# Expert layers in steps of four 32-row tiles instead of two 64-row tiles

## What is computed

```python
def hierarchical_moe(h, rg_w, rg_b, re_w, re_b, w_gate, w_up, w_down):
    x = h.reshape(-1, d)
    ...   # top-1 of 4 groups, then top-2 of 8 experts in it: two experts of 32 per token
    hid = silu(einsum("nd,edf->nef", x, w_gate)) * einsum("nd,edf->nef", x, w_up)
    out = einsum("nef,efd->nd", hid * gate[:, :, None], w_down)
```

```
layer 0: 53 32 38 22 37 29 30 35 31 33 37 30 32 28 38 25 18 16 17 23 19 24 13 20 61 58 50 58 56 81 79 61
layer 1: 53 10 35 32 36 28 17 19 15 43 64 5 21 14 54 10 44 15 7 146 78 50 118 192 7 8 1 7 24 5 4 22
```

## Time and profile before

| what | value |
|---|---|
| median of 3 runs | 1208.25 us (1205.42 to 1208.59) |
| span of the profiled execution, first to last instruction | 1203.8 us |
| PE, DVE, ACT, POOL busy | 87%, 53%, 29%, 18% of the span |
| expert part of layer 0 | from 283.5 us (tables ready) to 552.1 us (last result copied) |
| expert part of layer 1 | from 896.6 us to 1166.3 us |

### The profile page before, as it was taken

The page is one execution under the profiler, slowest core; times in us unless marked ns, Lnnn a source line. Parts: engine busy times, 40 slices in busy tenths (PEclk is TensorE's granted clock), DMA queues, the critical chain, the costliest instruction groups (busy, mean ns, idle before and its releaser), DMA issues.

```text
span 1203.8 us, 16465 instructions
## 1 busy us (share of the span) xinstructions
PE 1043.0 (87%) x5263; PEld 620.6 (52%) x5263; DVE 637.2 (53%) x1133; ACT 353.8 (29%) x548; POOL 213.0 (18%) x343
## 2 busy tenths in 40 slices
PE   7999998973997878798999899889928997799997
PEld 6999997851332322234677677655413332333342
DVE  2323326566453444262559999773383644455626
ACT  3231225112342333240322132460022433334420
POOL 5333334000121111112400000000001121122130
PEclk9999999995999888899999899999968998999998
DMA  9451202059999999985604121300299999999945
GB/s 286 124 170 71 71 1 108 36 231 376 364 414 406 377 394 412 401 317 221 222 17 140 30 71 64 106 14 35 95 378 377 403 411 390 402 399 372 367 162 210
DMA packets 74652, 284.19 MB, mean 236 GB/s; under 512 B 15787, under 2 KB 34431, under 8 KB 48831
## 3 DMA queue, kind: packets, MB, share of 16 engines
q1 hardware_dynamic: 58312, 242.63, 52.3%
q10 hardware_dynamic: 5383, 20.85, 5.0%
q0 software_dynamic: 10912, 20.10, 4.5%
HBM read 273.53 MB, written 27.26 MB: 250 GB/s over the span
## 4 chain that ended last, share of the span: by engine, by line
PE 57%; DMA 20%; DVE 13%; issue 3%; SPq 2%; ACT 2%; ACTq 0%; DVEq 0%; POOL 0%; POOLq 0%
PE ps L1118 14%; PE ps L1315 12%; DMA ring<-in_moe_w_down_dram 11%; DMA ring<-in_moe_w_up_dram 6%; PE ps L1134 6%; PE ps L1330 6%; PE ps L1166 5%; PE ps L1150 5%; PE ps L1243 3%; DVE arena L1906 2%; DVE ring L1906 2%; PE ps L1301 2%; PE ps L1418 1%; DMA arena<-x_rows_dram,now 1%; SPq L516 1%
## 5 line engine op out<-in xcount | busy, mean ns | idle before, releaser
L1315 PE MATMUL ps<-arena 128*64 128x512 f32 x1152 | 273.2, 630 | 41.0 <-DVE arena L1765 38.8
L1315 PEld LDWEIGHTS ps<-arena 128*64 128x64 f32 x1152 | 87.2, 145 | 222.4 <-issue 159.2
L1764 DVE COPY arena<-ring 128x1024 f32 x144 | 99.0, 687 | 114.4 <-SPq L593 70.0
L1330 PE MATMUL ps<-arena 128*64 128x512 f32 x576 | 131.5, 598 | 21.2 <-DVE arena L1781 21.2
L1134 PE MATMUL ps<-arena,ring 128*128 128x296 f32 x512 | 134.0, 424 | 7.1 <-DVE arena L1884 4.7
L1118 PE MATMUL ps<-hT_hi,w_hi 128*128 128x296 f32 x384 | 116.7, 304 | 7.6 <-PE ps L1118 6.7
L1134 PEld LDWEIGHTS ps<-arena,ring 128*128 128x128 f32 x512 | 99.6, 196 | 39.6 <-DVE arena L1884 5.2
L713 ACT COPY arena<-ring 128x1024 f32 x72 | 75.1, 1043 | 140.6 <-SPq L593 62.0
L1118 PE MATMUL ps<-hT_hi,w_lo 128*128 128x296 f32 x384 | 115.2, 300 | 0.0
L1118 PE MATMUL ps<-hT_lo,w_hi 128*128 128x296 f32 x384 | 115.1, 300 | 0.0
L1765 DVE COPY arena<-ring 128x1024 f32 x144 | 98.6, 685 | 0.0
(11 more groups left out here) (288 smaller groups left out, 1295.3 us busy)
## 6 DMA issues: line engine op xcount, KB each, us to landing
ring<-in_moe_w_gate_dram SPq DMA_DIRECT2D x64, 1024.0 KB, 7.9
ring<-in_moe_w_up_dram SPq DMA_DIRECT2D x64, 1024.0 KB, 10.2
ring<-in_moe_w_down_dram SPq DMA_DIRECT2D x64, 1024.0 KB, 10.5
ring<-in_sc_w_in_dram SPq DMA_DIRECT2D x12, 1024.0 KB, 12.2
ring<-y_rows_dram ACTq DMA_DIRECT2D x6, 1024.0 KB, 6.9
ring<-in_cf_w_pw_dram SPq DMA_DIRECT2D x4, 1536.0 KB, 15.5
ring<-in_sc_w_out_dram SPq DMA_DIRECT2D x2, 2048.0 KB, 7.9
x_rows_dram<-ring ACTq DMA_DIRECT2D x8, 512.0 KB, 2.6
```

The costliest lines, as they stand in the source:

```text
L1315: ins = nc.tensor.matmul(ps[own, B_GU, :], xT_e[:, k, own], w_gu[:, x, c, i * 2 * F:(i + 1) * 2 * F], start=(k == 0), stop=(k == C - 1))
L1330: ins = nc.tensor.matmul(ps[own, B_Y + half, :], hidT[:, k, own], w_dn[:, x, k, half * DH:(half + 1) * DH], start=(k == 0), stop=(k == FK ...
L1764: nc.vector.tensor_copy(as_gu(w_gu[:, 0, c, :]), gu_chunk(ranks[0], c))
```

## The change

A tile has at most 32 rows and a step has four tiles ("quads"), one for each quarter of the array's columns: 13 steps in layer 0 and 14 in layer 1. The staging area is now three rotating buffers, each holding one chunk for all four tiles; a step has six chunks (four of gate and up, two of down), and a chunk can be staged when the chunk three before it has been used. VectorE stages three tiles of gate and up, tile 0 of the first down chunk and tiles 0 and 1 of the second; ScalarE stages the rest, the last two down copies behind the silu and the copy of the next step's x. VectorE copies a step's result after the third chunk of the next step. The gate and up weights are loaded by halves (four transfers of 512 KB, then 1 MB of down): the first half of a slot is free when chunks 0 and 1 of the last step that needs its expert are staged, the second half after chunks 2 and 3, the down part after both down chunks. The router's tables grow with the number of tiles (`TAB` 72 for 56, `CAP` 19 for 10), and an early expert always counts one tile.

The sizes and the staging buffers:

```diff
     R = P // 2
-    TILES = (PAIRS - E) // R + E
-    NDUO = -(-TILES // 2)
-    CAP = -(-T // R)
-    TAB = 56
-    assert TILES + 4 <= TAB <= P and PAIRS > 4 * P and TAB % 2 == 0
+    PER = 4
+    RT = P // PER
+    TILES = (PAIRS - E) // RT + E
+    NQUAD = -(-TILES // PER)
+    CAP = -(-T // RT)
+    TAB = 72
...
+        CHUNK = PER * UNIT
+        STAGED = 3
+        staged = arena[:, 0:STAGED * CHUNK].rearrange("p (b x n) -> p b x n", b=STAGED, x=PER)
...
+        CHUNKS = NCH + FK
+        BUFFER_OF = (2, 0, 1)
...
+        def buffer_of(c):
+            return staged[:, BUFFER_OF[c % STAGED]]
+
+        AHEAD = 5
```

The loads (`load_expert` on SP) and their waits:

```diff
+                for half in range(2):
                     if upto is not None:
-                        if part is down:
-                            wait_down_copied(layer, upto)
-                        else:
-                            wait_gate_up_copied(layer, upto)
-                    for dst, src in part:
-                        sp.dma_start(dst, src, **cond).then_inc(slot_loaded[r % SLOTS], 16)
-
-            def wait_gate_up_copied(layer, upto):
-
-                sp.wait_ge(gu_ready[layer], NCH * ((upto + 1) // 2) + 1)
-
-            def wait_down_copied(layer, upto):
-
-                sp.wait_ge(dn_ready[layer], FK * ((upto + 1) // 2) + 1)
-
-            def wait_copied(layer, upto):
-
-                wait_gate_up_copied(layer, upto)
-                wait_down_copied(layer, upto)
+                        wait_gate_up_staged(layer, upto, half)
+                    at = half * KC * F
+                    for first, src in ((0, gate), (u, up)):
+                        sp.dma_start(s[:, first + at:first + at + KC * F], src[:, at:at + KC * F], **cond
+                                     ).then_inc(slot_loaded[r % SLOTS], 16)
+                if upto is not None:
+                    wait_down_staged(layer, upto)
+                sp.dma_start(s[:, 2 * u:3 * u], down, **cond).then_inc(slot_loaded[r % SLOTS], 16)
...
+            def wait_staged(layer, upto, chunks):
+
+                steps_over = (upto + (PER - 1)) // PER
+                sp.wait_ge(dve_staged[layer], steps_over * CHUNKS + (chunks - CHUNKS + AHEAD))
+                sp.wait_ge(act_staged[layer], steps_over * CHUNKS + (chunks - CHUNKS + AHEAD))
```

ScalarE's step:

```diff
+                    ranks = record(mybir.EngineType.Activation, s, 1, 3)
+                    act.wait_ge(weights_ready, ranks[2] + (SEQ_EXP[l] + 1))
+                    for c in range(NCH):
+                        if first and c == STAGED:
+                            copy_xT(0)
+                        if not first or c >= STAGED:
+                            act.wait_ge(chunk_used[l], CHUNKS * s + (c + 1))
+                        stage_gate_up(s, ranks[2], c)
+                    act.wait_ge(chunk_used[l], CHUNKS * s + (NCH + 1))
+                    stage_down(s, ranks, 0, (1, 2, 3))
+                    act.wait_ge(chunk_used[l], CHUNKS * s + (NCH + STAGED))
                     if not first:
                         act.wait_ge(hid_done[l], s)
                     nc.scalar.activation(silu_sb, ps[:, B_GU, 0:F], ACT.Silu).then_inc(silu_done[l], 1)
                     if not final:
                         copy_xT(s + 1)
-
-                act.sem_inc(dn_ready[l], 1)
-                copy_dn(0, record(mybir.EngineType.Activation, 0), True)
-                last = last_duo(act)
-                copy_xT(0)
+                    stage_down(s, ranks, 1, (2, 3))
```

TensorE's gate and up product:

```diff
+                        pe.wait_ge(dve_staged[l], CHUNKS * s + (c + 1 + AHEAD))
+                        pe.wait_ge(act_staged[l], CHUNKS * s + (c + 1 + AHEAD))
                         for i in range(2):
                             k = 2 * c + i
-                            for x in range(2):
-                                own = slice(x * R, (x + 1) * R)
+                            for x in range(PER):
+                                own = slice(x * RT, (x + 1) * RT)
                                 ins = nc.tensor.matmul(ps[own, B_GU, :], xT_e[:, k, own],
-                                                       w_gu[:, x, c, i * 2 * F:(i + 1) * 2 * F],
+                                                       buffer_of(c)[:, x, i * 2 * F:(i + 1) * 2 * F],
                                                        start=(k == 0), stop=(k == C - 1))
-                        ins.then_inc(gu_used[l], 1)
+                        ins.then_inc(chunk_used[l], 1)
```

VectorE's step:

```diff
+                def stage_gate_up(s, ranks, c):
+
+                    for x in range(3):
+                        if c == 0:
+                            dve.wait_ge(weights_ready, ranks[x] + (SEQ_EXP[l] + 1))
+                        last = nc.vector.tensor_copy(as_gu(buffer_of(c)[:, x, :]), gu_chunk(ranks[x], c))
+                    last.then_inc(dve_staged[l], 1)
...
+                def body(s, before=None, second=False):
+
+                    first = before is None
+                    ranks = record(mybir.EngineType.DVE, s, 0, 3)
+                    for c in range(NCH):
+                        if not first or c >= STAGED:
+                            dve.wait_ge(chunk_used[l], CHUNKS * s + (c + 1))
+                        stage_gate_up(s, ranks, c)
+                        if c == STAGED - 1 and not first:
+                            copy_y(before, second)
+                    for k, tiles in enumerate(((0,), (0, 1))):
+                        dve.wait_ge(chunk_used[l], CHUNKS * s + (NCH + k + 1))
+                        stage_down(s, ranks, k, tiles)
+                    multiply(s, first)
```

More of the change, by code:

```diff
@@ new lines, in load_expert @@
+                down = w_down[layer, e1].rearrange("e (p k) d -> p (e k d)", k=FK)
+                for half in range(2):
+                    if upto is not None:
+                        wait_gate_up_staged(layer, upto, half)
[3 more added lines that the diff above has]
+                                     ).then_inc(slot_loaded[r % SLOTS], 16)
@@ new lines, in load_expert, with wait_gate_up_staged @@
+                if upto is not None:
[5 more added lines that the diff above has]
+                sp.wait_ge(act_staged[layer], steps_over * CHUNKS + (chunks - CHUNKS + AHEAD))
+            def wait_gate_up_staged(layer, upto, half):
+                wait_staged(layer, upto, NCH // 2 * (half + 1))
@@ L531, in pass_on, with wait_down_staged @@
+            def wait_down_staged(layer, upto):
+                wait_staged(layer, upto, CHUNKS)
             def pass_on(n):
@@ L978, in _ @@
                 nc.gpsimd.tensor_copy(dst, dst.bitcast(I32)).then_inc(iota_made, 1)
-            for dst, by in ((steps, R), (evens, 2)):
+            for dst, by in ((steps, RT), (fours, PER)):
                 step(nc.gpsimd.iota(dst[:].bitcast(I32), pattern=[[by, dst.shape[1]]], base=0, channel_multiplier=0))
@@ L1038, in experts @@
                 pool.wait_ge(tab_ready, l + 1)
-                last = last_duo(pool)
+                last = last_quad(pool)
                 pool.wait_ge(x_turned[l], 1)
@@ L1282, in rank @@
                     for part in range(2):
-                        last = nc.tensor.matmul(ps[:, B_IDS, 0:NDUO], r_low[:, i, :], r_high[:, part, i, :],
+                        last = nc.tensor.matmul(ps[:, B_IDS, 0:NQUAD], r_low[:, i, :], r_high[:, part, i, :],
                                                 start=(i == 0 and part == 0), stop=(i == 2 * NT - 1 and part == 1))
@@ L1294, in experts @@
                 pe.wait_ge(tab_ready, l + 1)
-                last = last_duo(pe)
+                last = last_quad(pe)
                 def turn_x(s):
@@ L1756, in experts, with stage_down @@
                 dve.wait_ge(tab_ready, l + 1)
-                def copy_gu(s, ranks, first):
-                    dve.wait_ge(weights_ready, ranks[1] + (SEQ_EXP[l] + 1))
-                    for c in range(NCH):
-                        if not first:
-                            dve.wait_ge(gu_used[l], NCH * s + (c - NCH + 1))
-                        nc.vector.tensor_copy(as_gu(w_gu[:, 0, c, :]), gu_chunk(ranks[0], c))
-                        nc.vector.tensor_copy(as_gu(w_gu[:, 1, c, :]), gu_chunk(ranks[1], c)).then_inc(gu_ready[l], 1)
+                def stage_gate_up(s, ranks, c):
[4 more added lines that the diff above has]
+                    last.then_inc(dve_staged[l], 1)
+                def stage_down(s, ranks, k, tiles):
+                    for x in tiles:
+                        last = nc.vector.tensor_copy(buffer_of(NCH + k)[:, x, :],
+                                                     down_chunk(ranks[x], k).rearrange("p s n -> p (s n)"))
+                    last.then_inc(dve_staged[l], 1)
                 def copy_y(s, first):
-                    dve.wait_ge(dn_used[l], FK * s + (FK + 1))
+                    dve.wait_ge(chunk_used[l], CHUNKS * s + (CHUNKS + STAGED))
                     if not first:
@@ L1860, in _ @@
             combine(0)
[L1862 removed]
+            dve.wait_ge(y_stored[0], (last_quad(dve) + 1) * 16)
```

148 lines of the change are left out of this document (69 added, 79 removed).

## The result

The changed kernel takes 1274.7 us (median; 1273.0 to 1278.7) against 1206.8 beside it: ratio 1.0581, 95% interval 1.0534 to 1.0628. Measured a second time it was 1278.3, ratio 1.0607 (1.0574 to 1.0640). The direction was right, the size was not: I had 31.7 us, it is about 70. The time sits at the edge of the range.

A forecast was written before the change was run, and what follows sets the result against it. Loads were taken to bound layer 0, with a tail of steps, and layer 1 up to expert 19, then PE. Layer 0's 20.8, layer 1's 9.4 and the router's 1.5 us added 31.7 to 1208.25: 1240, range 1217 to 1275.

The forecast's parts named there:

- What bounds the kernel: Both expert parts: loads bound layer 0 with a tail of steps, layer 1 up to expert 19, then PE.
- The gap is 1.4 at most … I take 1.: Load stream at each step of four different experts: idle 1.4 us at most, nothing at least, 1 taken.
- SP's issues hidden behind 8.6 us of load: Load queue: SP's two more issues per expert, 0.35 us each, hide behind the load and cost nothing.
- The start: Start of each layer's loads: expert 10 lands 6.4 us late in layer 0 and 10.8 us late in layer 1.
- 4 KB packets: Gate and up loads by halves: smaller packets cost 0.2 us an expert, with 0 as the other bound.
- The step: One step on PE: 13.5 us from start to start against 12.55 before, bounds 12.55 and 14.5.
- the rival of 0.86: PE's array runs only two quarters at a time, 0.86 us a group, 22.9 a step, 1320 us in all; chance 0.07.
- estimated 0.54: In-between rival on PE's array: a group of four quarters takes 0.54 us, a quarter longer, 1269 us in all; chance 0.10.
- The ends: Last steps of each expert part: layer 0 ends 20.8 us later, layer 1 9.4 us later.
- The router: Router's wider tables in both layers: about 0.75 us a layer on the path, 1.5 us in all.
- the starts are not covered: Denies the rival that queued work from early experts covers both layers' late starts, giving 1223 us; chance 0.11.
- the fewer steps don't pay: Denies the rival that eight steps behind expert 19 shorten layer 1 by 20 us, giving 1204 us; chance 0.08.

The follow-up runs named there:

- e11: Expert 11, not a run; its first gate load goes out 59.6 us after the tables in layer 0 before, 71.0 changed.
- e15: Expert 15, not a run; at the profiled step of experts 10 to 13 its down part goes out at 401.9 us.
- e16: Expert 16, not a run.
- e22: Expert 22, not a run.
- e23: Expert 23, not a run.
- e26: Expert 26, not a run; in layer 1 the forecast has expert 31 need its slot.
- e27: Expert 27, not a run.
- e7_even: Changed kernel with each expert's number of 32-row tiles rounded up to even, so a step holds two experts at most: 1264.7 us, ratio 1.0500.
- e5: Expert 5, not a run; before the change its gate load in layer 0 goes out at 291.18 us.
- e10: Expert 10, not a run; before the change it landed at 348.9 us in layer 0 and 957.8 in layer 1.
- e9: Expert 9, not a run.
- e5_before_halves: Kernel before the change, with each gate and up load cut in two halves and no wait changed: 1216.0 us, ratio 1.0104.
- e4_whole: Changed kernel with gate and up loaded whole, each when all four gate and up chunks are staged: 1263.6 us, ratio 1.0482.
- e2_y_later: Changed kernel with VectorE's copy of the last step's result put behind the copies of chunk 3: 1268.7 us, ratio 1.0535.
- e28: Expert 28, not a run; the forecast has it land at 516.5 us in layer 0, with four steps behind it.
- e19: Expert 19, not a run; it landed at 1036.0 us in layer 1 before, forecast 1049.6.
- e31: Expert 31, not a run; its first gate load goes out 230.8 us after the tables in layer 0 before, 259.1 changed.
- e10_before_three_halves: Kernel before, staged as if with three rotating chunk buffers, gate and up in halves each freed by its own two chunks: 1240.4 us, ratio 1.0303.

## Why the prediction was right in direction and wrong in size

**What bounds the kernel**: right. The parts are bound by the loads, fewer steps don't shorten them, and what counts is when the stream starts and whether it stops.

**The step that failed: "The gap is 1.4 at most … I take 1."** The time of release was right to 1 us (14.8 against 13.9). The queue was not: I let it move at its full rate until the last byte and again from the first. The trace shows the share sink over 12 us and come back over 8. Two terms of the working were too small. I let a down part that goes out into the drained queue land 1.3 + 2.6 = 3.9 us after its release; it took 7.4 (401.93 to 409.3), and 6.8 to 7.4 at all seven such places of this trace, the two starts and five steps of four experts. Two of them stand on the chain:

```profile
466.59 6.88 DMA ring<-in_moe_w_down_dram
...
505.13 7.26 DMA ring<-in_moe_w_down_dram
```

And I had SP's issues hidden behind 8.6 us of load. SP issues in order, so at such a step the next expert's loads stand behind the wait and go out from 404.86 to 407.18, 2.9 to 5.3 us after the down part, with only that 1 MB of weights queued until then. How much each adds was not separated.

At a step of four experts 4.5 us are lost in share. Against before, the first gate load of an expert is 12.0 us late on average from e11 to e15, 17.2 from e16 to e22, 22.8 from e23 to e26 and 28.2 from e27 on (10.6, 13.1, 17.6 and 23.3 in the second profile): about 4 to 5 at each of the three steps, packets included. In e7_even it is 9.8, 9.6, 10.5 and 13.0. In layer 0 the way from e11 to e31 became 12 to 17 us longer; I had 7, packets included.

**The start**: the same step, in another place. SP's three issues for e5 came 1 to 1.5 us after the times that I had (290, 300 and 308.4):

```profile
291.52 0.37 SPq L523 DMA_DIRECT2D ring<-in_moe_w_gate_dram  x1
...
301.46 0.34 SPq L523 DMA_DIRECT2D ring<-in_moe_w_gate_dram  x1
...
309.46 0.33 SPq L527 DMA_DIRECT2D ring<-in_moe_w_down_dram  x1
```

From there I had the down part landed at 312.3, and it landed at 316.3. The idle share from 285 to 320 adds up to 12.6 us (0.36 x 15 + 0.36 x 20), and the stream is 11 us late at e11, where I had 6.4 at e10. In layer 1 it is 21 late, against 10.8. 13 of these remain in e7_even, which has no step of four different experts; the other 8.5 are gone there, most of them with the step of experts 5 to 8, for which I had 1: in the changed kernel the lag is 15.0 when e9 has landed and 20.1 when e10 has.

**4 KB packets**: 0.2 us an expert was about right for the stream in layer 0 (0.17), but the 6 that it put into the sum (21 and 9 experts) are half of the 12.5 (e5_before_halves) and 13.5 (e4_whole) that whole loads save.

**The step**: the four quarters do run together, 7.41 / 16 = 0.46 us for a group of four, where I took 0.43 from two halves; the rival of 0.86 is out. By the Trainium skill (TensorE: Matmul & The Clock Gate, Part 3, Measured speedup vs the span model) I had estimated 0.54 from its three tiles; the trace doesn't agree, four tiles lost less here. A step takes 14.3 us, not 13.5, inside the bounds: "VectorE's 15 copies at 0.61 and its PSUM copies fit in that" left out that the result's copy stands ahead of chunk 3. e2_y_later took it away and got 13.55 and 7 us.

**The ends**: in layer 0 the four steps behind e28 took 61.0 us (531.7 to 592.7) instead of 55.3. In layer 1 the five from e19 on took 73.2 (1095.08 to 1168.25) instead of 67.5, the slots of e28 to e31 came that much later, and the end moved by 32, not 9. The chain's end is the one I had written down. From e31's first load to the last copy layer 0 takes 50.0 and 50.8 us, 37.9 before. So the three terms of layer 0 were all too small: the start 6.4 for 11, the stream 7.2 for 12 to 17, and what follows it 7.2 for 12 to 13.

**The router**: 1.5 us were not seen. The tables are ready at 283.61 us in layer 0, at 283.48 before. The time between the two expert parts is 5 us shorter than before in both profiles of the changed kernel (339.6 against 344.5); over all the profiles it lies between 339.5 and 344.7, and why, no run tells.

**Rivals**: the starts are not covered, and the fewer steps don't pay: from e19 to e27, where the loads of layer 1 wait for steps, the lag shrinks only from 23.3 to 21.3 us (23.5 to 23.3 in the second profile).

The 70 us, by e10_before_three_halves and e7_even, if their parts add up: some 36 are the half-staged step and the halves (17.0 of them in layer 0, 15.2 in layer 1). Of the rest, in layer 0, 4 come with quarters as such (from the one run to the other), no more than such a length is good to, and 15 to 20 with more than two experts in a step. In layer 1 the rest is 17 to 20, and e7_even can't split it. How much of a late release is PE's cold clock (gate and up take 9.13 us where PE has waited 11.9 us before, at a granted clock of 0.50 from 388 to 392, which is 1.2 GHz, against 7.41 in a step without a pause) was not tried.

## What to carry to other kernels

A ring of slots that feeds a load-bound part is sized by what one step holds and by how late it lets go: a step of four experts in a ring of five leaves one load to cover the whole step. Before widening a step, work out the release of each slot from the landing of its last expert, and count a pause of the stream as the time it takes to sink and to come back, not as the dry time alone; here that was 4.5 us where the sum had 1. Cutting loads to free buffers earlier is worth it only where the early part is really waited for; here whole loads were 13.5 us faster.

## What the runs showed of the hardware

GpSimd's copy of one column of 128 indices takes 0.18 us in every step before (x36, 177 to 184 ns). In the changed kernel it takes up to 3.49 us, and it ends with VectorE's run of copies: at 1118.45 (1114.96 + 3.49), where that run ends at 1118.41 (1116.52 + 1.89). By the Trainium skill (SBUF — State Buffer, SBUF: two separate sides) these two engines share a port pair, and one of them holds it for a whole instruction; here GpSimd was kept out over six copies in a row. It delays the result's store. At the end of layer 0 such a copy (581.87, 3.48 us) is on the chain that ended last, but GpSimd's work behind it is over at 592.69 and the last result's copy at 592.66, so it cost nothing that can be seen.

After a pause the loads come back slowly: 253 and 292 GB/s in the two stretches of 4 us behind SP's issue at 401.93, then 429. Part of the first is SP's order, by which no weights but 1 MB are queued until 404.86. From 408 to 412 all of e16's loads are queued and the share is 0.96, and the rate is still 292; why, no run tells.
